# HGRN heads of a two-block model: the head pipeline made one iteration deeper, four PSUM copies moved to ScalarE, one multiply per level

## The reference

```
q, f, i, g = split(h @ w_in, 4)            # h = rmsnorm(x), four products of 1024x1024x1024
k  = (1 - lb) * sigmoid(-f);  log_f from f and lb;  q = silu(q) / sqrt(128);  v = i
S_t = diag(f_t) S_{t-1} + k_t v_t^T        # per head, a 128x128 state
o_t = S_t^T q_t
o = o * rsqrt(mean(o*o, per head) + eps);  y = o * out_norm * silu(g);  mix = y @ w_out
```

## Time and profile before

| | us |
|---|---|
| device time, median of 3 runs | 2515.36 (2514.09 to 2518.74) |
| span of the profiled execution, first to last instruction | 2511.6 |
| PE busy | 2444.9 (97%) |
| PE weight load busy | 2038.0 (81%) |
| DVE busy | 1118.2 (45%) |
| POOL busy | 742.1 (30%) |
| ACT busy | 417.4 (17%) |

### The profile page before, as it was taken

One profiled execution on the slowest core, in us unless ns is written; L12 is line 12 of the kernel. 1 busy time (PEld: TensorE's weight loads), 2 busy tenths in 40 slices (PEclk: granted clock), 3 DMA queues, 4 the chain that ended last, 5 costly groups with the idle time before them and its releaser, 6 DMA issues.

```text
span 2511.6 us, 29616 instructions
## 1 busy us (share of the span) xinstructions
PE 2444.9 (97%) x11520; PEld 2038.0 (81%) x11520; DVE 1118.2 (45%) x1449; ACT 417.4 (17%) x691; POOL 742.1 (30%) x420
## 2 busy tenths in 40 slices
PE   7999999899999999999999999999999999999998
PEld 5778888788888888888888888888888888888886
DVE  7777777865321221221366666555421131221233
ACT  4222222212210210200231002002220120110210
POOL 2121111233333333333332222333233333332331
PEclk9999999999999999999999999999999999999999
DMA  3101010022111111111111111111111111111112
GB/s 134 34 27 33 25 33 25 26 100 67 42 50 50 50 44 49 50 50 46 46 50 67 34 42 43 42 42 51 42 50 45 48 50 50 48 44 50 50 50 75
DMA packets 36639, 123.05 MB, mean 49 GB/s; under 512 B 4704, under 2 KB 4832, under 8 KB 36576
## 3 DMA queue, kind: packets, MB, share of 16 engines
q1 hardware_dynamic: 35568, 120.54, 15.0%
q10 hardware_dynamic: 1008, 1.62, 0.2%
HBM read 117.95 MB, written 4.19 MB: 49 GB/s over the span
## 4 chain that ended last, share of the span: by engine, by line
PE 90%; DVE 6%; DVEq 2%; issue 1%; ACT 1%; DMA 0%; SPq 0%; ACTq 0%
PE prod_ps L377 27%; PE prod_ps L379 27%; PE prod_ps L378 27%; DVE hgrn_qk L888 2%; PE side_ps L507 2%; PE side_ps L423 2%; PE side_ps L429 1%; DVEq L895 1%; PE side_ps L437 1%; PE side_ps L447 1%; PE side_ps L439 1%; DVE sq_sum L791 1%; DVE x_res L1140 1%; DVE hgrn_scores L914 0%; PE side_ps L456 0%
## 5 line engine op out<-in xcount | busy, mean ns | idle before, releaser
L377 PE MATMUL prod_ps<-operand_hi,w_hi 128*128 128x512 f32 x3264 | 1289.6, 395 | 12.3 <-DVE operand_lo L795 11.8
L379 PE MATMUL prod_ps<-operand_hi,w_lo 128*128 128x512 f32 x3264 | 1276.1, 391 | 0.0
L378 PE MATMUL prod_ps<-operand_lo,w_hi 128*128 128x512 f32 x3264 | 1275.5, 391 | 0.0
L377 PEld LDWEIGHTS prod_ps<-operand_hi,w_hi 128*128 128x128 f32 x3264 | 616.5, 189 | 139.6 <-POOL w_lo L325 8.9
L379 PEld LDWEIGHTS prod_ps<-operand_hi,w_lo 128*128 128x128 f32 x3264 | 615.5, 189 | 130.3
L378 PEld LDWEIGHTS prod_ps<-operand_lo,w_hi 128*128 128x128 f32 x3264 | 616.5, 189 | 123.9
L323 POOL CAST w_hi<-w_raw 128x1024 fp32r<-128x1024 f32 x200 | 208.0, 1040 | 1688.3 <-PE prod_ps L379 1682.9
L325 POOL TENSOR_TENSOR w_lo<-w_raw,w_hi 128x1024 fp32r<-128x1024 f32 x200 | 516.2, 2581 | 16.0
L1092 DVE SCALAR_TENSOR_TENSOR work<-prod_ps,inv_rms 128x512 f32<-128x512 f32 x128 | 88.4, 692 | 493.3 <-PE prod_ps L379 492.7
L1104 DVE TENSOR_TENSOR x_res<-prod_ps,x_res 128x512 f32<-128x512 f32 x96 | 66.4, 691 | 432.9 <-PE prod_ps L379 432.9
L1510 ACT ACTIVATE work<-work 128x512 f32<-128x512 f32 x128 | 81.0, 633 | 1044.9 <-DVE work L1092 1044.9
(11 more groups left out here) (151 smaller groups left out, 1194.6 us busy)
## 6 DMA issues: line engine op xcount, KB each, us to landing
w_raw<-stream SPq DMA_DIRECT2D x204, 512.0 KB, 3.5
x_in<-x_t SPq DMA_DIRECT2D x16, 256.0 KB, 6.6
x_res<-x_t SPq DMA_DIRECT2D x8, 512.0 KB, 4.4
out_t<-x_res SPq DMA_DIRECT2D x16, 256.0 KB, 2.1
masks_f<-masks SPq DMA_DIRECT2D x1, 896.0 KB, 9.0
ret_rows<-head_rows ACTq DMA_DIRECT2D x1, 512.0 KB, 3.5
ret_cos<-rope ACTq DMA_DIRECT2D x1, 512.0 KB, 4.4
ret_sin<-rope ACTq DMA_DIRECT2D x1, 512.0 KB, 5.2
```

The source lines that it names most:

```text
L377: nc.tensor.matmul(prod_ps[:, bank], w_h, a_h, start=(k == 0), stop=False)
L378: nc.tensor.matmul(prod_ps[:, bank], w_h, a_l, start=False, stop=False)
L379: last = nc.tensor.matmul(prod_ps[:, bank], w_l, a_h, start=False, stop=(k == KT - 1))
```

## The change

The head pipeline becomes one iteration deeper. Iteration n now projects head n (units in the order v, f, q), runs levels L0 to L6 of head n-1, and L7, v, k, kv, T, o and back of head n-2. So ten iterations (0 to 9) take the place of nine, the last two with gate units in the place of projections. Two buffers each for v and scores are added. ScalarE takes v, k, o and back out of PSUM (for o it also squares straight from PSUM). `grow` does q and k in one TENSOR_TENSOR of 128x1024 in place of two of 128x512. `side_taken` becomes two semaphores, one for each PSUM pair, and TensorE waits for the step two before it on its own pair (`pair_free`), and for named ones (`taken_from`). SyncE's wait before unit 30 is now for TensorE's last `back`, of iteration 9.

```diff
-HG_ORDER = ("L3", "L4", "L5", "L6", "L7", "v", "k", "back", "kv", "T", "o", "L0", "L1", "L2")
+HG_ORDER = ("v", "L7", "L0", "k", "L1", "kv", "L2", "T", "L3", "o", "L4", "L5", "back", "L6")
...
-            sp.wait_ge(heads_done, 1)
+            sp.wait_ge(side_done, hgrn_step(HEADS1 + 1, "back") + 1)
...
+            def pair_free(step):
+                if not (isinstance(step, int) and step < 2):
+                    pe.wait_ge(side_taken[step_pair(step)], earlier_uses(step))
+                return step_pair(step)
...
+                def back():
+                    if older:
                         pe.wait_ge(o_normed, n - 1)
+                        turn(pair_free(hgrn_step(n, "back")), o_keep)
...
-                mids = [older_levels(3), older_levels(5), level7_and_v, chunk_kv, out, newer_levels(1)]
-                ends = [older_levels(4), older_levels(6), turn_k_and_back, turn_scores, after_fifth, newer_levels(2)]
+                mids = [turn_v_and_last_level, turn_k, kv_then_second_level, lambda: newer_level(3), None,
+                        back_then_sixth_level]
+                ends = [lambda: newer_level(0), lambda: newer_level(1), turn_scores, out_then_fourth_level,
+                        lambda: newer_level(5), None]
...
-                    nc.vector.tensor_tensor(q2[:, :, 1], q2[:, :, 1],
-                                            dec[:, :, 0:1].to_broadcast([P, pairs, h]), ALU.mult)
-                    nc.vector.tensor_tensor(k2[:, :, 0], k2[:, :, 0],
-                                            dec[:, :, 1:2].to_broadcast([P, pairs, h]), ALU.mult
-                                            ).then_inc(level_fed, 1)
+                    grown = bass.AP(tensor=h_kq[b], offset=0,
+                                    ap=[[2 * S, P], [S + h, 2], [2 * h, pairs], [1, h]])
+                    other = bass.AP(tensor=h_d[number - 1], offset=1,
+                                    ap=[[2 * pairs, P], [-1, 2], [2, pairs], [0, h]])
+                    nc.vector.tensor_tensor(grown, grown, other, ALU.mult).then_inc(level_fed, 1)
```

More of the change, by code:

```diff
@@ L120, in ret_step, with step_number, step_pair, earlier_uses @@
             at -= 1
-    return n * len(RET_ORDER) + (T_RET + at), pair
+    return n * len(RET_ORDER) + T_RET + at if isinstance(n, int) else (n, len(RET_ORDER), T_RET + at)
+def step_number(step):
+    if isinstance(step, int):
+        return step
+    n, stride, first = step
+    return n * stride + first
+def step_pair(step):
+    return (step if isinstance(step, int) else step[2]) % 2
+def earlier_uses(step, back=0):
+    if isinstance(step, int):
+        return (step + back) // 2
+    n, stride, first = step
+    return n * (stride // 2) + (first + back) // 2
 def build(nc, stream, x_t, gains, conv_w, lower_bound, head_rows, head_scalars, rope, ident_in, ones_in, masks_in, out_t):
@@ L546, in out, with newer_level @@
[L546 to L558, removed]
+                def newer_level(number):
+                    if newer:
+                        level(number, n - 1, prev)
@@ L568, in hgrn_iteration @@
                     product(uu, slot, half, 0, mid=mids[j])
-                    ends[j]()
+                    if ends[j] is not None:
+                        ends[j]()
             def x_count(k, half):
@@ L585, in _ @@
             hgrn_iteration(0, 0, mid_start=True)
-            hgrn_iteration(1, 1)
-            with pe.Fori(1, HEADS1 // 2) as i:
+            for n in range(1, 4):
+                hgrn_iteration(n, n % 2)
+            with pe.Fori(2, HEADS1 // 2) as i:
                 hgrn_iteration(i * 2, 0)
@@ L591, in _ @@
             hgrn_iteration(HEADS1, 0)
[L592 to L597, removed]
+            hgrn_iteration(HEADS1 + 1, 1)
+            units(U_G1, HEADS1 // 2, 0, 3)
             late_start(U_OUT1, 1, by_tile_then_half(u_ready, 16), [[]] * 4)
@@ L965, in hgrn_iteration @@
[L965 to L971 removed]
+                    step = hgrn_step(n, "kv")
+                    kv = done_step(step).rearrange("p (c v) -> p c v", c=NB)
                     nc.vector.tensor_copy(h_state[:, 1], kv[:, 0])
@@ L1013, in hgrn_iteration @@
                 third(5)
-                if project:
-                    dve.drain()
-                    dve.sem_inc(v_t_ready, 1)
-                    level(par, 2)
-                if gates_now:
-                    normed(n + 1)
-            hgrn_iteration(0, 0)
-            hgrn_iteration(1, 1)
-            with dve.Fori(1, HEADS1 // 2) as i:
+            for n in range(4):
+                hgrn_iteration(n, n % 2)
+            with dve.Fori(2, HEADS1 // 2) as i:
                 hgrn_iteration(i * 2, 0)
@@ L1170, in ret_states @@
                         ALU.mult, ALU.add)
-                last.then_inc(side_taken, 1)
+                last.then_inc(taken(step), 1)
                 dve.drain()
@@ new lines, in take_back, with hgrn_iteration @@
+            def take_back(n):
+                step = hgrn_step(n, "back")
+                o_at = ho[:, n - 2] if isinstance(n, int) else ho[:, bass.ds(n - 2, 1)].rearrange("p a s -> p (a s)")
+                nc.scalar.activation(o_at, done_step(step), ACT.Copy).then_inc(taken(step), 1)
+                act.drain()
+                act.sem_inc(heads_back, 1)
+            def hgrn_iteration(n, par):
+                static = isinstance(n, int)
+                newer, older = not (static and not 1 <= n <= HEADS1), not (static and not 2 <= n <= HEADS1 + 1)
@@ L1440, in hgrn_iteration, with f_sigmoids @@
-                older(4)
-                q_sigmoid(0)
-                older(5)
-                if not (isinstance(n, int) and n < 2):
-                    root(n, one_norm)
-                older(6)
-                q_sigmoid(1)
-                older(7)
-                for half in range(NH):
+                def f_sigmoids(half):
                     act.wait_ge(evac, g + (half + 3))
@@ L1487, in advance @@
+            take_o(HEADS1 + 1)
+            gate_high(8)
+            gate_sigmoid(9)
+            root(HEADS1 + 1, one_norm)
+            gate_high(9)
+            gate_sigmoid(10)
+            take_back(HEADS1 + 1)
+            gate_high(10)
+            for j in range(11, 2 * HEADS1):
+                gate_sigmoid(j)
+                gate_high(j)
             def advance(u0, make_operand, gain_row, with_gain=False):
```

432 lines of the change are left out of this document (236 added, 196 removed).

## The result

| | before | after |
|---|---|---|
| device time, median | 2515.36 us (9 runs, 2512.52 to 2518.74) | 2522.93 us (9 runs, 2518.23 to 2527.87) |
| span of the profiled execution | 2511.6 us | 2517.8 us |

The change made the kernel slower, by 0.3%: ratio 1.0028, 95% interval 1.0018 to 1.0038, or 7 us. The forecast was 2528. The busy line of the page after, which answers to the earlier trace rows, shows the work moved as intended: VectorE has 50 us less, ScalarE 30 us more, TensorE the same number of instructions.

A forecast was written before the change was run, and what follows sets the result against it. TensorE, busy 97% of the span, was taken as the bound, with at most 47 us to gain in the HGRN stage. Removed 48.6 and added 61.4 give +12.8, so 2528 us; forecast's own range 2517 to 2536, overall 2504 to 2541.

The forecast's parts named there:

- The sum of what was added: New TensorE waits from the deeper order, 51.2 us, with the lower clock 61.4 us.
- `back`: TensorE waits before `back` for `normed`, queued on VectorE behind level 5: 3.5 us in iterations 2 to 7, 21.2 in all.
- L2: TensorE waits 1.7 us before L2, as GpSimd's lock delays L1's copies; with 0.25 before T, 11.7 us over six iterations.
- unit 30: TensorE waits 4.9 us before unit 30's first matmul, because SyncE may not load it before the last `back`.
- the clock: Low clock on TensorE after the new waits: six times 1.7 us, 10.2 us, bounds 2 and 15.
- The chain: VectorE's queue from L5's last issue through level 5, p4's evacuation and two scalings to `normed` and `back`: 6.35 us.
- The second half of the term: T waits 0.25 us more for its PSUM pair, after VectorE empties a bank and runs the states.
- Iteration 1: No kv stands between L1 and L2, so TensorE comes earlier to L2 and waits 3.2 us.
- Iteration 8: Gate work in VectorE's queue: waits of 1.7 us before L2, 2.5 before T, 5.2 before `back`, together 9.4.
- Iteration 9: No levels but L7 there: 0.8 us of waiting, as an estimate.
- What went: All 25 HGRN-stage waits 40.4 us, their low clock 6.8, fewer cuts in TensorE's products 1.4: -48.6 us.
- The parts said to be neutral: Merged multiply gains 0.06 us per level; the four copies moved to ScalarE do nothing for the queue ahead of `back`.

The follow-up runs named there:

- Experiment 1: Changed kernel with VectorE doing `normed` right after `norm_factor`, before level 5, not behind it: 2493.09 us, ratio 0.9906 to the kernel before.
- Experiment 3: Changed kernel with each level's decay product moved behind the masked copies on VectorE: 2503.99 us, ratio 0.9947 to the kernel before.
- experiment 12: Changed kernel with GpSimd splitting the units of the heads one product later, away from level 1: 2535.86 us, ratio 1.0087 to the kernel before.
- experiment 4: Changed kernel with `normed` earlier, units 30 and 31 loaded earlier, masked copies first, and L7's gather ahead of a gate copy: 2471.10 us, ratio 0.9818.
- Experiment 2: Changed kernel with SyncE loading units 30 and 31 before it waits for the last `back`: 2513.99 us, ratio 0.9990 to the kernel before.
- experiment 6: Changed kernel with VectorE again taking v, k, o and back out of PSUM: 2526.47 us, ratio 1.0048 to the kernel before.

## Why the prediction was right, and where its terms were off

The sum of what was added came out nearly exact, 61.4 predicted against 61.6 (41.5 of idle time, 0.17 for each of the 18 waits, half of the 34 us of low clock). The main mechanisms are those that I named: `back`, L2, unit 30 and the clock. That the sum agrees this well is luck: the waits came out 6.6 us lower than I had them (44.6 for 51.2) and the clock 6.9 higher (17.1 for 10.2). From there to the time: the stage came out 3.9 shorter than the sum (last point but one), the rest of the span 2.7 shorter, and the median lies 5.1 above the span where I took 3.8: 12.8 - 3.9 - 2.7 + 1.3 = 7.5. The last 1.3 is the clock too: the profiled execution had a mean clock of 0.990, and the one with the median time 0.988 and a span of 2521.0.

- **`back`.** Predicted 3.5 in each of iterations 2 to 7; measured 2.89 idle, 3.1 with the gap. The chain took 5.91 us from L5's last issue (299.90) to `back` (305.81), against 6.35. I charged 0.89 for the evacuation with the gap behind it, but that gap is only there when what follows waits for TensorE; with a scaling behind it it is 0.60 (302.55 to 303.15). The hand-over was 0.05, not 0.20. Experiment 1 shows the step itself.
- **L2.** Predicted 1.7; 1.35 idle, 1.5 with the gap. The two durations worked out from one row of the lock, 3.25 for the subtraction and 2.87 for the product behind it, were met to 0.07 us (4.70 less 1.45 is 3.25, 5.25 less 2.45 is 2.80). Experiment 3 shows that it is this product that holds the copies off, and experiment 12 that GpSimd's split holds the product. The Trainium skill says (SBUF — State Buffer, § Who interferes with whom) that a VectorE instruction with two SBUF inputs contends with a GpSimd instruction that reads SBUF, under an exclusive lock. The trace agrees, with the 3.25 and 2.87 us here and the 0.69 of experiment 12. The second half of the term, 0.25 before T, did not come in iterations 2 to 7.
- **Iteration 1.** 3.2 predicted, 0 measured. I took it that L2 needs L1's pair of banks. In iteration 1 the order has no kv, so L2 stands two places behind L0, not L1, and uses L0's pair. The timeline of TensorE shows L1 and L2 half a product apart:

```profile
65.18 1.07 PE L533 MATMUL side_ps<-hgrn_kq,hgrn_mixed 128*128 128x128 f32 x8
...
68.86 1.07 PE L533 MATMUL side_ps<-hgrn_kq,hgrn_mixed 128*128 128x128 f32 x8
```

- **Iteration 8.** 1.7 + 2.5 + 5.2 predicted; 1.4 for L2, 1.9 for T, at most 4.1 for `back`.
- **Iteration 9.** 0.8 predicted as an estimate. A wait of 3.0 us came before L7, and 0.67 before `back`: a gate multiply was locked by the split (2.86 us against 0.75), and the gather of L7 stood behind what ScalarE makes of it. I had not followed ScalarE's queue there. Moving the gather ahead of that one item (experiment 4) left 3.3 us of waiting, so this item is not the whole cause.

```profile
485.57 2.86 DVE L868 SCALAR_TENSOR_TENSOR g_in<-g_in,gain,sig 128x512 f32<-128x512 f32 x1
```

- **Unit 30.** 4.9 predicted, 5.1 measured. Experiment 2 shows it. (My terms add up to 7.8 and not 7.7, so 5.0.)
- **The clock.** 10.2 predicted, 17 measured. This is the term that I sized worst: there were seven low stretches for my six, and in iterations 7 and 8 and at unit 30 the clock stayed at 0.50 for 6.8 us and not 3.4. Why it stayed down longer there, no run shows. The trace does not agree with a low stretch at each gap, which the Trainium skill's rule (TensorE: Matmul & The Clock Gate, § HAM oscillation) would make of it: iterations 3 and 5 had the same waits of 2.8 to 2.9 us before `back` as 2, 4 and 6 and no low clock. These waits are shorter than the 3.5 us that I had put under that rule.
- **What went.** All 25 waits, as forecast, but the balance is some 4 us off: 61.6 added less 48.6 gives +13.0 for the stage, and it was +8.9. Two sources can be seen. The low stretches after lie partly over waiting, where they cost nothing: TensorE is busy in 29.4 of their 34 us, so they cost 14.7 and not 17. One of them, by the windows:

```profile
250.20:253.60 3.40, 2.95 (x14) 2.95 (x15) 0.40 (x1) 0.84 (x1) 0.00 (x0) 0.50 0.00 0
```

  And the level behind a wait takes 0.9 us from start to start and not 0.81 (in both kernels), 0.1 us per wait for 7 waits fewer. Together 3 of the 4 us, by subtraction; no experiment took them apart, and the last one is open.
- **The parts said to be neutral.** The merged multiply takes 1.226 us in the mean of 48 (1.23 taken), the PSUM copies of 128x1024 on ScalarE 1.00 to 1.03 (bounds 1.0 to 1.3). That the four copies "do nothing for this chain" held in iterations 2 to 7, and to 2 us of waiting in the last two (experiment 6).

What I had not seen is how near the other sign was: one call, moved by one level, makes 22 us less than before out of 7 more.

## What to carry to other kernels

A deeper pipeline doesn't remove waits; it gives each result a new deadline, and one result whose producer stands behind the wrong item in an engine's queue can turn the gain into a loss. So list for each hand-over when it is wanted and what its producer has queued ahead, and place it by its deadline: here that was worth 52 us at the new depth, and one of its edits, tried at the old depth, nothing. Judge an offload by what it moves out of a locked or late place, not by its microseconds: 3.7 us per iteration gave 1 to 3 us in all, and another 1.2, ahead of a lock, gave 22.

## What the runs showed of the hardware

- The same waits draw the low clock in some iterations and not in others, and for 3.4 or 6.8 us. After, iterations with the same waits take 53.7 us at a clock of 1.00 and 55.0 to 56.6 with low stretches; experiment 2, with the same waits in the head pipeline, shows 6.8 us of it in iteration 3. Removing waits gave more than their sum (19 us for 9.5, 30 for 22), in good part because the low clock went with them. Iterations 2 and 5 of the kernel after, by the windows:

```profile
92.50:147.50 55.00, 50.84 (x289) 44.18 (x289) 36.06 (x54) 16.40 (x28) 11.61 (x6) 0.97 0.09 29
256.60:310.40 53.80, 49.55 (x290) 42.93 (x290) 35.55 (x53) 16.39 (x28) 11.09 (x6) 1.00 0.10 30
```

- The price of the lock doesn't depend on the size of the operation caught, but on how much of GpSimd's is left: 2.37 us for 128x32 and 2.87 for 128x512 (0.19 and 0.69 alone), both started 0.92 us into the subtraction; the 128x512 of experiment 3 started 2.05 into it and took 1.75. In all three it ended only behind the subtraction, by 0.06, 0.54 and 0.55 us. Masked copies from PSUM, with a mask in SBUF, run beside the same subtraction unharmed (1.33 for two).
- A multiply over two halves with a step of -1 between its decays takes as long as the plain one of that size: 1.23 us for 128x1024.
